# A new order in a fused kernel's pooling stage: two scalings change engines, and six unread products stand among the gate's units

## The reference, cut to what matters

```python
sh1, sc1, g1, sh2, sc2, g2 = ada_mods(c, ada_w, ada_b)   # silu(c) @ ada_w + ada_b, ada_w is 1024 x 6144
u = modulate(rms_norm(x, mix_pre_g), sh1, sc1)
y = pool_mixer(u, pool_w, pool_scale)   # per group of 256 channels: (window mean - itself) @ pool_w[g], times pool_scale
x = x + g1 * rms_norm(y, mix_post_g)
f = conv_ffn(modulate(rms_norm(x, ffn_pre_g), sh2, sc2), ffn_w_up, ...)
```

## Time and profile before

| what | us |
|---|---|
| median of 3 runs (lowest, highest) | 1145.45 (1145.17, 1146.87) |
| the profiled execution | 1145.39 |
| its span, first to last instruction | 1143.6 |
| PE busy in it | 1122.1 (98%) |
| first product of the feed-forward part starts at | 78.87 |

### The profile page before, as it was taken

One profiled execution on the slowest core, in us unless ns is written; L12 is line 12 of the kernel. 1 busy time (PEld: TensorE's weight loads), 2 busy tenths in 40 slices (PEclk: granted clock), 3 DMA queues, 4 the chain that ended last, 5 costly groups with the idle time before them and its releaser, 6 DMA issues.

```text
span 1143.6 us, 17120 instructions
## 1 busy us (share of the span) xinstructions
PE 1122.1 (98%) x6830; PEld 917.8 (80%) x6830; DVE 549.7 (48%) x882; ACT 497.0 (43%) x690; POOL 455.0 (40%) x348
## 2 busy tenths in 40 slices
PE   7999999999999999999999999999999999999997
PEld 4668888888888888888788878888888888888886
DVE  3572554334452235567986556422200443676825
ACT  3374553544422223875443245745322343534632
POOL 1115544445455371654432211034354444564430
PEclk9999999999999999999999999999999999999999
DMA  9994232332342333434232211222333322223201
GB/s 342 416 355 141 74 110 77 107 110 73 110 121 85 111 111 112 148 103 119 74 96 90 75 37 38 74 74 74 104 129 111 111 79 86 100 75 112 74 1 74
DMA packets 87240, 128.97 MB, mean 113 GB/s; under 512 B 13300, under 2 KB 66306, under 8 KB 86919
## 3 DMA queue, kind: packets, MB, share of 16 engines
q1 hardware_dynamic: 81730, 119.62, 31.0%
q10 hardware_dynamic: 5445, 8.42, 2.1%
HBM read 122.77 MB, written 5.26 MB: 112 GB/s over the span
## 4 chain that ended last, share of the span: by engine, by line
PE 86%; DVE 6%; issue 3%; DMA 2%; ACT 2%; POOL 1%; SPq 1%; DVEq 0%; POOLq 0%
PE ps L295 24%; PE ps L297 24%; PE ps L296 24%; PE ps L1801 3%; DVE conv_v L1336 2%; DMA ada<-in_ada_w 1%; PE ps L2340 1%; DVE diag L1386 1%; PE ps L2341 1%; PE ps L2409 1%; DVE shift_acc L1110 1%; PE ps L2399 1%; POOL wl L443 1%; PE ps L2346 1%; DVE outer L1383 1%
## 5 line engine op out<-in xcount | busy, mean ns | idle before, releaser
L443 POOL TENSOR_TENSOR wl<-raw,wh 128x512 fp32r<-128x512 f32 x312 | 419.6, 1377 | 611.9 <-ACT wh L501 611.9
L295 PE MATMUL ps<-xth,wh 128*128 128x512 f32 (+1 forms) x832 | 324.5, 390 | 1.1 <-DVE xtl L1233 0.7
L297 PE MATMUL ps<-xth,wl 128*128 128x512 f32 (+1 forms) x832 | 317.5, 382 | 0.0
L296 PE MATMUL ps<-xtl,wh 128*128 128x512 f32 (+1 forms) x832 | 317.2, 381 | 0.0
L501 ACT ACTIVATE wh<-raw 128x2048 fp32r<-128x2048 f32 x78 | 149.3, 1914 | 303.8 <-PE ps L297 280.8
L295 PEld LDWEIGHTS ps<-xth,wh 128*128 128x128 f32 x832 | 156.5, 188 | 33.8 <-issue 3.8
L297 PEld LDWEIGHTS ps<-xth,wl 128*128 128x128 f32 x832 | 156.4, 188 | 30.4
L296 PEld LDWEIGHTS ps<-xtl,wh 128*128 128x128 f32 x832 | 156.6, 188 | 28.9 <-issue 0.5
L1241 DVE SCALAR_TENSOR_TENSOR conv_out<-ps,conv_taps,conv_out 128x511 f32<-128x511 f32 x44 | 32.7, 744 | 124.7 <-ACT conv_out L668 124.7
L1336 DVE SCALAR_TENSOR_TENSOR conv_v<-ps,gdn_taps,conv_v 128x511 f32<-128x511 f32 (+2 forms) x96 | 71.8, 748 | 40.3 <-ACT conv_v L736 37.6
L295 PE MATMUL ps<-wh,xth 128*128 128x512 f32 x176 | 69.7, 396 | 0.0
(11 more groups left out here) (368 smaller groups left out, 1631.5 us busy)
## 6 DMA issues: line engine op xcount, KB each, us to landing
ada<-in_ada_w SPq DMA_DIRECT2D x24, 1024.0 KB, 12.8
raw<-in_gdn_w_in SPq DMA_DIRECT2D x24, 1024.0 KB, 5.3
raw<-in_ffn_w_up SPq DMA_DIRECT2D x22, 1024.0 KB, 5.0
raw<-in_gla_w_in SPq DMA_DIRECT2D x12, 1024.0 KB, 5.1
raw<-in_ffn_w_down SPq DMA_DIRECT2D x11, 1024.0 KB, 4.9
raw<-in_gdn_w_out SPq DMA_DIRECT2D x8, 1024.0 KB, 4.9
raw<-in_gla_w_out SPq DMA_DIRECT2D x4, 1024.0 KB, 5.0
xres<-in_x SPq DMA_DIRECT2D x4, 512.0 KB, 5.1
```

The costliest lines, as they stand in the source:

```text
L295: nc.tensor.matmul(o, lh, rh, start=first, stop=False)
L296: nc.tensor.matmul(o, lh, rl, start=False, stop=False)
L297: return nc.tensor.matmul(o, ll, rh, start=False, stop=last)
L443: rest = nc.gpsimd.tensor_tensor(lo[:, part], raw[:, s, part], hi[:, part].bitcast(f32), ALU.subtract)
```

## The change

The order of the norms becomes y0, y1, y2, u0, u1, y3, u2, u3. POOL no longer scales the mixer weights; DVE does so before its shift sums. DVE no longer scales the normed residual; ACT does (`norm_scale`). The copies of the turned tiles 0 and 1 go from ACT to DVE, where they stand before `gain_sum(0)`. The shift's columns and rows use bank 1 instead of banks 2 and 3, so that the third tile's products (`mixed_group(2, g)`) need not wait for them and are moved among the gate's units. Two times three unread products stand beside the gate's last two units, and the last group of unread products has four instead of six. The first two units of the fourth chunk move ahead of the fourth tile's products. On PE the turned tiles and the gain's units change places.

```diff
-NORM_ORDER = (("y", 0), ("y", 1), ("u", 0), ("y", 2), ("u", 1), ("y", 3), ("u", 2), ("u", 3))
+NORM_ORDER = (("y", 0), ("y", 1), ("y", 2), ("u", 0), ("u", 1), ("y", 3), ("u", 2), ("u", 3))
...
-            pool.wait_ge(S("pool_in"), 32)
-            pool.wait_ge(S("vec_done"), 2)
-            for part in range(2):
...
             pool.wait_ge(S("mods_done"), 3)
             nc.gpsimd.memset(g2_acc[:], 0.0).then_inc(S("g2_zero"), 1)
...
-            def turned_copy(tt):
...
+            def norm_scale(tt):
+
+                act.wait_ge(S("inverse_done"), 2 + NORM_ORDER.index(("u", tt)))
+                act.wait_ge(S("pool_mm"), 1 + KD)
+                nc.scalar.activation(xn[:, tt, :], xres[:, tt, :], ACT.Copy, scale=stat[:, 2, tt:tt + 1]).then_inc(S("xn_done"), 1)
+
+            for tt in range(2):
+                norm_square("y", tt)
+                norm_root("y", tt)
             high(0, 0, 0)
-            norm_square("y", 1)
-            norm_root("y", 1)
+            norm_square("y", 2)
+            norm_root("y", 2)
             norm_square("u", 0)
-            norm_square("y", 2)
             norm_root("u", 0)
-            norm_root("y", 2)
+            norm_scale(0)
             norm_square("u", 1)
             norm_root("u", 1)
             norm_square("y", 3)
             norm_root("y", 3)
+            norm_scale(1)
             act.wait_ge(S("ada_used"), 12)
...
             nc.scalar.activation(ada_part[:, 1, :], ps[:, 1, :], ACT.Copy).then_inc(S("ada_summed"), 1)
             norm_square("u", 2)
             norm_root("u", 2)
+            norm_scale(2)
             norm_square("u", 3)
             norm_root("u", 3)
-            for tt in range(TT - 1):
-                turned_copy(tt)
+            norm_scale(3)
+            act.wait_ge(S("turned"), 3)
+            act.wait_ge(S("pooled_written"), 2)
+            nc.scalar.activation(pooled[:, :, 2 * P:3 * P], bank2(4).rearrange("p (k n) -> p k n", n=P), ACT.Copy).then_inc(S("pooled_written"), 1)
...
+            def scale_weights(part):
+
+                v.wait_ge(S("pool_in"), 32)
+                g = slice(2 * part, 2 * part + 2)
+                V.tensor_tensor(pool_w[:, g], pool_w[:, g],
...
             mod_col(1, 3, SC1, PRE1)
+            v.wait_ge(S("vec_done"), 2)
+            for part in range(2):
+                scale_weights(part)
             for k in range(KD):
                 shift_sum(k)
...
+            norm("y", 0)
             ada_sum(2)
-            norm("y", 0)
+            norm("y", 1)
             v.wait_ge(S("mod_mm"), 4)
             V.tensor_tensor(g1_row[:], bank2(0), post1_row[:], ALU.mult).then_inc(S("mods_done"), 1)
             v.wait_ge(S("mods_done"), 3)
             add_mixed(0)
-            norm("y", 1)
+            norm("y", 2)
             add_mixed(1)
-            scale_normed(0)
-            norm("y", 2)
+            norm("u", 0)
             add_mixed(2)
-            scale_normed(1)
+            norm("u", 1)
             norm("y", 3)
             add_mixed(3)
-            scale_normed(2)
+            norm("u", 2)
+            turned_out(0)
+            norm("u", 3)
+            turned_out(1)
             gain_sum(0)
-            scale_normed(3)
             mod_col(3, 1, SH2)
             gain_col(0)
             gain_sum(1)
             turned_out(3)
...
             ada_unit(2, 0)
+            mixed_group(2, 0)
             pe.wait_ge(S("mods_done"), 2)
...
             mm.then_inc(S("mod_mm"), 1)
+            mixed_group(2, 1)
             ada_unit(2, 1)
             mixed_shift(0)
             mixed_shift(1)
+            keep_busy(3, 1)
             ada_unit(2, 2)
-            mixed_group(2, 0)
-            mixed_group(2, 1)
+            keep_busy(3, 1)
             ada_unit(2, 3)
             mixed_group(2, 2)
             mod_row(2, 0)
             mixed_group(2, 3)
             mixed_shift(2)
+            ada_unit(3, 0)
+            ada_unit(3, 1)
             mixed(3)
             mixed_shift(3)
-            for n in range(4):
-                ada_unit(3, n)
+            ada_unit(3, 2)
+            ada_unit(3, 3)
             turn_normed(0)
+            turn_normed(1)
             gain_unit(0, 0)
-            gain_unit(0, 1)
             mod_col(3, 1, 0)
             mod_col(3, 1, 1)
-            turn_normed(1)
+            gain_unit(0, 1)
+            turn_normed(2)
             gain_turn(0)
-            turn_normed(2)
+            turn_normed(3)
             gain_unit(1, 0)
             gain_unit(1, 1)
-            turn_normed(3)
             gain_turn(1)
             pe.wait_ge(S("pooled_written"), 2)
-            keep_busy(6, 3)
+            keep_busy(4, 3)
```

More of the change, by code:

```diff
@@ L1160, in norm @@
                 inverse(stat[:, 1 if what == "y" else 2, tt:tt + 1])
[L1162 to L1166, removed]
+            def scale_weights(part):
+                v.wait_ge(S("pool_in"), 32)
+                g = slice(2 * part, 2 * part + 2)
+                V.tensor_tensor(pool_w[:, g], pool_w[:, g],
+                                pool_scale_row[:].rearrange("p (g n) -> p g n", n=GDIM)[:, g].unsqueeze(2)
+                                .broadcast_to([P, 2, GDIM // P, GDIM]), ALU.mult).then_inc(S("pool_in"), 1)
             def add_mixed(tt):
@@ L1177, in turned_out @@
                 v.wait_ge(S("turned"), tt + 1)
-                v.wait_ge(S("pooled_written"), tt)
                 V.tensor_copy(pooled[:, :, tt * P:(tt + 1) * P],
@@ L1187, in _ @@
             mod_col(1, 3, SC1, PRE1)
+            v.wait_ge(S("vec_done"), 2)
+            for part in range(2):
+                scale_weights(part)
             for k in range(KD):
                 shift_sum(k)
-            mod_col(0, 2, SH1)
+            mod_col(0, 1, SH1)
             v.wait_ge(S("mod_mm"), 3)
-            V.tensor_copy(shift_row[0:64, 0, :], ps[0:64, 3, 0:GDIM])
-            V.tensor_copy(shift_row[0:64, 1, :], ps[64:128, 3, 0:GDIM]).then_inc(S("cols_done"), 1)
+            V.tensor_copy(shift_row[0:64, 0, :], ps[0:64, 1, GDIM:2 * GDIM])
+            V.tensor_copy(shift_row[0:64, 1, :], ps[64:128, 1, GDIM:2 * GDIM]).then_inc(S("cols_done"), 1)
+            norm("y", 0)
             ada_sum(2)
-            norm("y", 0)
+            norm("y", 1)
             v.wait_ge(S("mod_mm"), 4)
@@ L1904, in mixed_group @@
                 if tt == 2 and g == 0:
-                    pe.wait_ge(S("mods_done"), 2)
-                    pe.wait_ge(S("cols_done"), 7)
+                    pe.wait_ge(S("mods_done"), 1)
                 if tt == 3 and g == 0:
@@ L1975, in _ @@
                 for c in range(0, P, 32):
-                    mm = X.matmul(ps[c:c + 32, 2, k:k + 1], shift_acc[:, k * P + c:k * P + c + 32], ones[:, 0:1], start=True, stop=True)
+                    mm = X.matmul(ps[c:c + 32, 1, k:k + 1], shift_acc[:, k * P + c:k * P + c + 32], ones[:, 0:1], start=True, stop=True)
             mm.then_inc(S("mod_mm"), 1)
             ada_unit(2, 0)
+            mixed_group(2, 0)
             pe.wait_ge(S("mods_done"), 2)
```

2 lines of the change are left out of this document (1 added, 1 removed).

## The result

The changed kernel takes 1148.34 us (median of 20 runs, 1144.55 to 1152.02), the kernel before 1146.12 beside it (20 runs, 1143.34 to 1147.67): ratio 1.0025 [1.0015, 1.0034], or 2.9 us slower (1.7 to 3.9). The forecast was 1146.5, no change.

The account below looks back on a forecast made before the run. PE, with 86% of the last-ending chain, bounds the kernel, so the start's end counts: +1.5 at the last copy, including the gate's 0.2 gain, less 0.4 overlap, gives +1.1; 1145.39 + 1.1 = 1146.5, range 1143.6 to 1148.4.

Parts of the forecast that it names:

- Full clock gives back 3.61 - 1.86 = 1.75: Gate's stretch on PE: with the six unread products the clock stays full, so four products take 1.75 us less.
- the size of the gate's stretch: PE from the shift to the gate's row: 13.93 + 2.7 - 1.75 - 0.3 = 14.6 us, ending 0.2 earlier.
- The filled wait of 0.3: PE's 0.3 us wait for `shift_row` in the gate's stretch is filled by a moved group of products and saved.
- The 0.9 of the mixer weights: DVE before the shift: with the weights' scaling moved from POOL, the shift sums end 0.9 us earlier, at 39.4.
- Six products on the path, 2.7.: Gate's stretch on PE: the six new unread products add 2.7 us, with ends of 0 and 2.9.
- The rival by which they are hidden: PE would have waited for the gate's last load, so the six products cost nothing: -2.7, 1143.8 alone; chance 0.10.
- DMA gap and load wait gone.: Units 18 and 19 load some 7 us earlier; the gap at 62 to 65 and PE's wait at 73.07 go, up to 3 us.
- ACT's queue becomes the link.: In the norms, ACT's scalings (1.1 each), squares and roots set the fourth inverse, at 70.8 against 70.28.
- The rival of hidden scalings: ACT's scalings do not queue ahead of the squares; the fourth inverse comes 2.1 us earlier, 1144.4; chance 0.14.
- DVE's order costs the tail.: `turned_out(1)`, 1.22, now stands before `gain_sum(0)` on DVE; the last copy ends at 78.05 against 76.57, +1.5 us.
- The rival of the clock's fall in the hole: PE's clock falls after its 2 us wait behind the third turn; about 1.7 us more, 1148.2; chance 0.22.
- The rival by which the six products don't hold the clock: In the gate's stretch the clock falls despite the six products: +1.75 us, 1148.2; chance 0.08.

Follow-up runs that it names:

- e7: The kernel before with only the two times three unread products added beside the gate's units; 1149.01 us, ratio 1.0026.
- e3: The changed kernel with unread products added in PE's waits for the shift sums (three) and after the third turn (four); 1148.97 us, ratio 1.0029.
- e13: The kernel before with only the fourth chunk's first two units moved ahead of the fourth tile's products; 1143.15 us, ratio 0.9983.
- e9: The changed kernel with DVE's first gain sum moved ahead of the copy of turned tile 1; 1147.00 us, ratio 1.0013.
- e4: The changed kernel with DVE's second gain sum moved behind the last turned tile's copy and the first modulation; 1145.45 us, ratio 1.0000.
- e6: The changed kernel with the scaling of the normed residual back on DVE; 1148.65 us, ratio 1.0030.
- e2: The changed kernel without its two times three unread products among the gate's units; 1144.44 us, ratio 0.9981.
- e8: The kernel before with only the mixer weights' scaling moved from POOL to DVE; 1145.19 us, ratio 0.9993.
- e1: The kernel before, unchanged, run and profiled again; 1145.14 us, ratio 0.9995.
- e5: The changed kernel without the six unread products and with the second gain sum behind the last turned tile's copy; 1142.49 us, ratio 0.9969.

## Why the prediction was wrong

**The step that failed** is "Full clock gives back 3.61 - 1.86 = 1.75". It credits to the six products a fall that one profile showed. Two things are wrong with it. The products don't hold the clock: 0.9943 with them, 0.9941 without (e7), and in the profiles of the changed kernel and of e3 it falls inside the gate's stretch all the same. And a fall seen once is not a fall in each run: the 131 runs of before have mean clocks from 0.989 to 0.999, and profiles of it and of its variants show falls at 13 to 15, at 45 to 47 or at 54 to 57, or at two of these. What the change gives back is the difference of the mean losses, 6.7 - 5.9 = 0.8, with a standard error of 0.4, and the falls ahead of the change are in it too. The filled wait alone gives more (e13, 6.7 - 5.1 = 1.6); what takes a part of that away in the changed kernel is not shown. The Trainium skill, "TensorE: Matmul & The Clock Gate", section "Part 1: The HAM clock gate (the "warmup" mystery)", says that how many matmuls one kernel runs at the low clock differs from run to run, and warns against fitting a model to one count. These runs agree, by the spread above; by that sentence the credit should not have been taken whole from one profile.

**The second step** is the size of the gate's stretch, which was too short even without a fall. The forecast has 14.6 from PE's start on the shift to the gate's row, 14.65 to `g_row`. Measured without a fall it is 15.70 (e9; e4 and e6 agree). Of the 1.05 between, 0.44 is the six products: 15.70 - 12.56 = 3.14 in place of 2.7, where the prediction's own upper end was 2.9. The other 0.61 is the new order. The working has 13.93 - 1.75 - 0.3, and 0.1 more to `g_row`: 11.95; the runs have 12.56 (e2), against 12.35 for the old order without a fall (e13, e8). The filled wait of 0.3 did not come back.

**The 0.9 of the mixer weights** stays open. Its mechanism holds: DVE's two operations are slow only beside POOL's, and end with POOL's (27.25 + 1.10 = 28.35 in e1, POOL at 28.33), which agrees with the rule of the Trainium skill, "SBUF — State Buffer", section "Who interferes with whom", that the prediction cites. That the first sum meets POOL hangs on when the weights' load lands, at 25.6 in the profile of before and at 23.7 in e1. Where it does not meet POOL, though, PE's first two tiles end later than the sums, and the move still brings PE's start forward, by 0.2 to 2.8 between any two of the profiles (e8). What this is worth in the mean over runs, e8's interval is too wide to say.

**The sum, redone.** The credit for the clock, 1.75 - 0.8 = 0.95, and the gate's 1.05: the forecast of +1.1 becomes +3.1; measured, +2.9 (1.7 to 3.9). The start on the shift (39.74, forecast 39.45) and the tail hold. That the two agree this well is in part luck, with 0.4 on the clock's term. By the rests: six products +2.9 (after against e2; 2.7 from e4 against e5, 3.3 from e7 against before), units -0.9 (e13), DVE's order in the tail +1.0 (e9), weights and gate order 0.0 and 0.2. That is 3.2 of the 3.5 between 1139.1 and 1142.7; the errors cover what is left.

The other points:
- *Six products on the path, 2.7.* The path is right, the size short by 0.44. The rival by which they are hidden is out.
- *DMA gap and load wait gone.* Right. I had seen the load and the wait, but not that the same two units raise PE's mean clock.
- *ACT's queue becomes the link.* The durations are right (1.15 against 1.1, the last inverse 16.25 behind the start of `g_row` against 16.65), and DVE does wait for ACT before it (1.32 at 73.11). But it is not the narrower queue: with the scaling back on DVE nothing is gained (e6), since DVE's queue is as long. The rival of hidden scalings, 1144.4, did not come.
- *DVE's order costs the tail.* Right: 23.36 without a fall (e3), 23.5 forecast, and 1.0 comes back when one line moves (e9).
- *The rival of the clock's fall in the hole* is what the profiled run did, at the place and with about the size described, 1.5 against 1.7. How often it comes over the runs is not shown.
- *The rival by which the six products don't hold the clock*, chance 0.08, has the mechanism right (e7), and its 1148.2 meets the measured 1148.3. The number is luck: its +1.75 again supposes a fall in each run of the changed kernel, and the rest of what is missing lies in the gate's 1.05.

Open: the mean clock is lower with the six products in the changed kernel (0.9949 against 0.9963, as much as e13's move gains, and 0.9953 against 0.9961) but not on the kernel before; why was not tried.

## What to carry to other kernels

A stall or a fall of the clock seen in one profile is a draw: before a change is credited with removing it, see whether other runs of the same kernel have it, and split mean time by mean clock. Unread products on an engine that only waits for itself cost their full time (3.14 in the profiles); here the clock gained where real work was moved into a wait (e13), and not where unread products were put into waits (e3). When one queue's work is moved to another, look which order the receiving and the giving queue have in the tail: one line on DVE was worth 1.0 to 1.3 (e9), another 2.2 to 2.9 (e4), by the rest and by the median.

## What was not expected of the hardware

The same kernel's time varies by 10.9 us in 131 runs (1141.7 to 1152.6), and it goes with the mean clock, 0.80 us for each 0.001. The kernels with a wait of 2.04 ahead of the fourth tile's products have a lower mean clock than the same kernels with real work in it (0.9941 against 0.9955, 0.9946 against 0.9968), whereas unread products in the two waits of e3 did not raise it. A fall of 6.8 us at 15 to 22 did not make PE later on the shift (40.04 in e1, 40.33 in the profile of before, which has no such fall).
